# A hybrid SSD / attention / MoE block in fp32: where mean squares are summed, in which order a norm's three small steps run, and how the router's logits are formed

## The chip, the cores and the metric

One NeuronCore of a Trainium2 chip runs the whole program; all arithmetic shown is fp32 unless marked bf16. The metric is the device time of one execution in microseconds. Engines are named as the profile does: PE is TensorE, DVE VectorE, ACT ScalarE, POOL GpSimd, and SP is SyncE, which here only issues DMAs.

## The reference, cut to what matters

Two layers work on 256 latent and 256 context tokens of width 1024. Layer 0 has an SSD (state space) mixer, layer 1 an attention mixer; each is followed by a mixture of experts with 16 experts, a shared expert and a router. Before every mixer and every MoE stands a norm with modulation, so there are four: layer 0 before SSD, layer 0 before MoE, layer 1 before attention (these three on 512 tokens), layer 1 before MoE (256 tokens).

```python
def rmsnorm(x, w):
    y = xf * lax.rsqrt(jnp.mean(xf * xf, axis=-1, keepdims=True) + EPS)
...
m_l = modulate(rmsnorm(h, norm2_w[l]), sh2, sc2)        # x * (1 + scale) + shift
h = h + g2 * grouped_moe(m_l, router_w, ...)
...
scores = jax.nn.sigmoid((t @ router_w).astype(jnp.float32))      # router_w is [1024, 16]
# group and expert choice from scores + bias, top 2 experts of a token
out = swiglu(t, sh_gate, sh_up, sh_down)                          # the shared expert
for e in range(N_EXPERTS):
    out = out + combine[:, e:e + 1] * swiglu(t, w_gate[e], w_up[e], w_down[e])
```

## The kernel before, in words

Activations lie transposed: `hT` (the residual) and `aT` (the normed input) are [128 channels, 8 blocks k, tokens]. Each engine has its own instruction stream, written out by hand, and they meet at semaphores only. Weights stream from HBM through ten slots of 1 MB, issued by SP in a fixed order; SP waits for a slot to be given back before it loads it again.

**A norm.** `norm_modulate` on ACT (L732) squares the eight blocks of `hT` into `aT` as they become ready (L737). `mean_square` on PE (L1052) multiplies each squared block by a 128x128 matrix of 1/1024 and sums the eight in one PSUM bank: eight fp32 matmuls of 128x512 (128x256 in the last norm), each shown as two instructions. `norm` on DVE (L1671) adds EPS out of PSUM (L1673) and takes the reciprocal (L1674); ACT takes the square root (L739); DVE multiplies each block of `hT` by the result (L1677), and ACT applies scale and shift per block (L744, one instruction for each 256 tokens), counted by `s_a`.

**What comes ahead of each norm.** Ahead of norm 1 (layer 0, MoE) PE projects the mixer's output in eight chunks m of 16 matmuls (L1297), and DVE adds each chunk to `hT` (L1878, L1880). Ahead of norm 3 (layer 1, MoE) it is the attention's output projection, L1614 and L2132. Ahead of norm 2 (layer 1, attention) the MoE's result is turned back by PE (L1431) and added to `hT` by DVE block by block (L2067); PE waits for all eight blocks (L1500) before it starts the eight mean-square matmuls in bank 7.

**The front of a MoE** (`moe_pe`, L1304; `moe_act`, L919; `moe_dve`, L2015). For each tile t of 128 tokens PE makes the router logits with eight matmuls: a block of `aT` is stationary (128x128), the router's 16 columns move (L1311). ACT takes the sigmoid (L932, with a table load), and DVE works through some fifty small linked steps, `route`, L1885, up to `s_sel`. Meanwhile PE runs the shared expert's `hidden_chunk(0, 0)` (gate in r = 0, up in r = 1, eight matmuls each, L1333) on weights that arrived long before, turns `aT` for the gathers (L1443), runs `hidden_chunk(0, 1)`, waits for `s_sel`, counts the ranks of the chosen tokens (L1451), and so on through two more chunks, between which DVE works out the order of the experts, a flag (L1972) and the gather indices (L1978 to L1991).

**After the front.** POOL gathers rows of tokens for each of the 16 experts, PE multiplies them in tiles of 32 rows in four column groups (L1379, L1409), and SP streams 6 MB of weights for each expert. In layer 0 SP loads no expert before the flag; in layer 1 one is loaded ahead, and the next when `hidden_chunk(0, 3)` gives the shared expert's slots back. After the last expert PE computes the shared expert's down projection (L1423).

Of the kernel before, what the change touches and what calls it, by code (L numbers as in the profile page):

```python
# [26 lines left out]
P = 128  # L27
# [176 lines left out]
def build(nc, a, out):  # L204
# [24 lines left out]
    with ExitStack() as ctx:  # L229
# [44 lines left out]
        cparts = sb("cparts", [P, 2, T], BF16)  # L274
        small = sb("small", [P, 16])
        ps = ctx.enter_context(nc.psum_tensor("ps", [P, 8, 512], F32))

# [99 lines left out]
        s_op, s_h1 = sem("out_proj"), sem("h_plus_mixer")  # L377
        s_rl, s_rs1 = sem("router_logits"), sem("router_sigmoid")
        s_gu, s_sg, s_hid, s_sd, s_hT, s_yn4, s_yu = (
# [213 lines left out]
        def _(pool):  # L593
            pool.memset(ones[:, :], 1.0).then_inc(s_set, 1)
            pool.memset(mean[:, :], 1.0 / D).then_inc(s_set, 1)
            pool.memset(cs[:, :, :], 0.0).then_inc(s_set, 1)

            pool.wait_ge(s_const, 16 * n_consts)
# [75 lines left out]
            def moe_pool(l):  # L674
# [6 lines left out]
                with pool.If(sparse):  # L681
# [14 lines left out]
                    for s in range(NE):  # L696
# [4 lines left out]
                        if s:  # L701
# [6 lines left out]
                            .then_inc(s_scat[l], 16)  # L708

            moe_pool(0)  # L710
            moe_pool(1)

        @block.scalar
        def _(act):
# [10 lines left out]
            act.wait_ge(s_par, 1)  # L725
            act.wait_ge(s_set, 3)
            act.activation(cs[:, :, 0:2], par[:, 296:312].rearrange("p (c k) -> p k c", c=2), ACT.Silu).then_inc(s_par, 1)
# [3 lines left out]

            def norm_modulate(l, m, n, ready):  # L732

                i = 2 * l + m
                for k in range(KD):
                    ready(k)
                    act.activation(aT[:, k, 0:n], hT[:, k, 0:n], ACT.Square).then_inc(s_sq, 1)  # L737
                act.wait_ge(s_rs, 2 * i + 1)
                act.activation(rstd[:, 0:n], rstd[:, 0:n], ACT.Sqrt).then_inc(s_rs, 1)  # L739
                act.wait_ge(s_mod, AMOD_N[l, m])  # L740
                for k in range(KD):
                    act.wait_ge(s_nx, KD * i + k + 1)
                    for q in range(n // S):
                        ins = act.activation(aT[:, k, q * S:(q + 1) * S], aT[:, k, q * S:(q + 1) * S], ACT.Identity,  # L744
                                             bias=mod[:, l, 24 * m + k, q:q + 1], scale=amod[:, l, m, k, q:q + 1])
                    ins.then_inc(s_a, 1)
# [6 lines left out]

            norm_modulate(0, 0, T, ready0)

# [15 lines left out]
            def conv_in(i):  # L771
                act.wait_ge(s_ip, i + 1)
                if i >= 2:
                    act.wait_ge(s_conv, i - 1)
                else:
                    act.wait_ge(s_set, 9)
                bank = i % 2 if i < AHEAD else 0
                act.copy(pre[i % 2][:, :, PADS:PADS + S], ps[:, bank, :].rearrange("p (s n) -> p s n", s=2)).then_inc(s_pre, 1)
# [140 lines left out]
            def moe_act(l):  # L919
                n = TOK[l]  # L920
                nt = n // P

                def chunk(e, f):
                    q = KF * e + f
                    act.wait_ge(s_gu[l], q + 1)
                    if q >= 2:
                        act.wait_ge(s_hid[l], q - 1)
                    act.activation(sg[f % 2][:, 0:n], ps[:, 2 * (f % 2), 0:n], ACT.Silu).then_inc(s_sg[l], 1)

                act.dma_start(valf[l], a["val"][l]).then_inc(s_val, 16)  # L930
                act.wait_ge(s_rl, l + 1)
                act.activation(rt[0][:, 0:nt * NE], ps[:, 6, 0:nt * NE], ACT.Sigmoid).then_inc(s_rs1, 1)  # L932
                chunk(0, 0)

                for r in range(2 * nt):
                    act.wait_ge(s_mt8, 8 * l + r + 1)
                    act.copy(mtok[:, r // 2, :].rearrange("p (k c q) -> p k c q", k=KD, c=KD)[:, :, 4 * (r % 2):4 * (r % 2) + 4, :],
                             ps[:, (4, 7)[r % 2], :].rearrange("p (c q k) -> p k c q", c=4, k=KD)).then_inc(s_mtv, 1)
                act.wait_ge(s_mtv, 8 * l + 2 * nt)
                act.dma_start(m_rows[0:n, :].rearrange("(t p) n -> p t n", p=P), mtok[:, 0:nt, :]).then_inc(s_mr, 16)  # L940
                for f in range(1, KF):
                    chunk(0, f)
                sparse = choose(act, l)
                with act.If(sparse):
                    rowsT_act(l, 0)
                    for s in range(NE):
                        tiled_act(l, s)
                    act.wait_ge(s_scat[l], 16 * NE)
                    act.wait_ge(s_dn[l], NE)
                    act.wait_ge(s_hT[l], NE)  # L950
                    pairs = y_rows[l].rearrange("(k t p) n -> p t k n", k=2, p=P)
                    for t in range(nt):
                        act.dma_start(ypair[:, t, :, :], pairs[:, t, :, :]).then_inc(s_yp[l][t], 16)
                with act.Else():
# [4 lines left out]
            norm_modulate(0, 1, T, lambda k: act.wait_ge(s_h1, k + 1))  # L959
            moe_act(0)  # L960

            norm_modulate(1, 0, T, lambda k: act.wait_ge(s_h2, k + 1))

# [36 lines left out]
            act.activation(esk, esk, ACT.Exp).then_inc(s_sum, 1)  # L1000
            norm_modulate(1, 1, S, lambda k: act.wait_ge(s_h1, KD + k + 1))
            act.dma_start(fnw, a["final_norm_w"].partition_broadcast(P)).then_inc(s_fw, 16)
# [12 lines left out]
        def _(pe):  # L1015
# [36 lines left out]
            def mean_square(i, n, bank):  # L1052
                for k in range(KD):
                    pe.wait_ge(s_sq, KD * i + k + 1)
                    ins = pe.matmul(ps[:, bank, 0:n], mean[:, :], aT[:, k, 0:n], start=(k == 0), stop=(k == KD - 1))  # L1055
                ins.then_inc(s_ms, 1)

            pe.wait_ge(s_set, 2)
# [159 lines left out]

            pe.wait_ge(s_set, 9)
            pe.wait_ge(s_cT, 3)  # L1220
# [67 lines left out]
            for m in range(KD):  # L1288
# [10 lines left out]
                if m == 0:  # L1299
                    pe.wait_ge(s_ssq, KI)  # L1300
                    pe.wait_ge(s_b3v, len(B3))
                    pe.matmul(ps[:, 3, :], mean[:, :], ssq[:, :], start=True, stop=True).then_inc(s_rsy, 1)

            def moe_pe(l):  # L1304
                n = TOK[l]
                nt = n // P
                for t in range(nt):
                    for k in range(KD):
                        if t == 0:
                            pe.wait_ge(s_a, KD * (2 * l + 1) + k + 1)  # L1310
                        ins = pe.matmul(ps[:, 6, t * NE:(t + 1) * NE], aT[:, k, t * P:(t + 1) * P], rw[:, k, :],  # L1311
                                        start=(k == 0), stop=(k == KD - 1))
                ins.then_inc(s_rl, 1)

# [8 lines left out]
                def hidden_chunk(e, f):  # L1323
# [7 lines left out]
                    for r in range(2):  # L1331
                        for k in range(KD):
                            ins = pe.matmul(ps[:, 2 * (f % 2) + r, 0:n], pair_slot(unit(e, k // 2))[:, k % 2, r, f * P:(f + 1) * P],  # L1333
                                            aT[:, k, 0:n], start=(k == 0), stop=(k == KD - 1))
# [159 lines left out]


            mean_square(1, T, 3)
            moe_pe(0)


            pe.wait_ge(s_h2, KD)  # L1500
            mean_square(2, T, 7)
            pe.wait_ge(s_a, 3 * KD)
# [102 lines left out]
            for m in range(KD):  # L1605
# [10 lines left out]
                ins.then_inc(s_ao, 1)  # L1616
            mean_square(3, S, 0)
            pe.wait_ge(s_h1, 2 * KD)
# [11 lines left out]
        def _(dve):  # L1630
# [48 lines left out]
            norm(0, T, 7)  # L1679
            ada_rows(0)  # L1680
# [190 lines left out]
            for m in range(KD):  # L1871
# [7 lines left out]
                for q in range(2):  # L1879
                    ins = dve.scalar_tensor_tensor(out=hT[:, m, q * S:(q + 1) * S], in0=yb[m % 2][:, q * S:(q + 1) * S],  # L1880
                                                   scalar=mod[:, 0, 16 + m, q:q + 1], in1=hT[:, m, q * S:(q + 1) * S],
                                                   op0=ALU.mult, op1=ALU.add)
                ins.then_inc(s_h1, 1)

            def route(l):  # L1885
# [15 lines left out]

                dve.wait_ge(s_rs1, l + 1)
                link(dve.tensor_tensor(e3(1), e3(0), rb[:, :].unsqueeze(1).to_broadcast([P, nt, NE]), ALU.add))
# [167 lines left out]

            norm(1, T, 3)
            moe_dve(0)

            norm(2, T, 7)

# [57 lines left out]
            norm(3, S, 0)  # L2134
            moe_dve(1)
# [34 lines left out]
```

## Time and profile before

| what | us |
|---|---|
| median of 3 runs | 1641.71 (1639.67 to 1646.81) |
| the profiled execution, own time | 1640.55 |
| its span | 1638.4 |
| PE busy | 1445.5 (88%) |
| DVE busy | 518.5 (32%) |
| ACT busy | 378.3 (23%) |
| POOL busy | 187.7 (11%) |

Shares by engine of the chain that ended last: PE 72%, SP's queue 9%, DMA 7%, DVE 5%, ACT 5%. The page also gives the clock that PE was granted in each fortieth of the span (a 9 is full speed or nearly; a 5 is half):

```profile
PEclk9599989999989999979999999997999899999987
```

The chain is followed back from the last instruction, at each step to what released it. So an engine that is busy but not in the chain costs nothing there, and the busy share says nothing about a single stage. The chain and the instructions in time are the views to read for a change that touches short stretches only.

### The profile page before, as it was taken

What the parts mean: (1) busy time and instruction counts of PE and PEld (TensorE: products, weight loads), DVE (VectorE), ACT (ScalarE), POOL (GpSimd) and SP (SyncE); (2) the same over time, 40 slices, a digit from 0 to 9 for tenths busy, and PEclk for the clock granted to TensorE, in tenths of its full rate; (3) what the DMA queues carried; (4) which work ended last, traced back from release to release, by engine and by line L of the source; (5) the groups of instructions that cost most, each with busy time, mean ns of one, the idle gap of its engine ahead of it and who ended that gap; (6) DMA issues with size and microseconds to landing.
All of it is one profiled execution on the core that took longest, in us unless ns stands there. A gap on an engine that the chain in (4) does not pass through costs nothing.

```text
span 1638.4 us, 28948 instructions
## 1 busy us (share of the span) xinstructions
PE 1445.5 (88%) x12440; PEld 832.2 (51%) x12440; DVE 518.5 (32%) x918; ACT 378.3 (23%) x900; POOL 187.7 (11%) x207
## 2 busy tenths in 40 slices
PE   4799989899988999899999998996988999988766
PEld 2433445454544444365555555552845775554424
DVE  3255555544443221224121121132244331211103
ACT  2211334333424210130121121113053212211111
POOL 0000033223242200000011111000000000111100
PEclk9599989999989999979999999997999899999987
DMA  7355314344340442003999999990400349999992
GB/s 280 126 183 202 128 65 149 125 139 141 120 138 26 110 122 77 26 25 129 389 370 373 384 392 381 378 323 2 142 26 4 116 139 352 393 397 399 403 392 100
DMA packets 128132, 334.46 MB, mean 204 GB/s; under 512 B 13123, under 2 KB 60923, under 8 KB 121851
## 3 DMA queue, kind: packets, MB, share of 16 engines
q1 hardware_dynamic: 116027, 308.76, 51.8%
q0 software_dynamic: 6144, 12.60, 2.3%
q10 hardware_dynamic: 5824, 11.16, 1.9%
q8 instruction: 101, 1.65, 0.4%
q14 instruction: 36, 0.29, 0.1%
HBM read 325.65 MB, written 14.68 MB: 208 GB/s over the span
## 4 chain that ended last, share of the span: by engine, by line
PE 72%; SPq 9%; DMA 7%; DVE 5%; ACT 5%; issue 2%; DVEq 0%; ACTq 0%; POOLq 0%
PE ps L1379 12%; PE ps L1085 10%; PE ps L1102 7%; PE ps L1297 7%; SPq L517 6%; PE ps L1409 5%; PE ps L1333 4%; PE ps L1036 3%; PE ps L1423 3%; SPq L519 2%; PE ps L1190 2%; DMA ssb<-in_moe_w_up 2%; PE ps L1614 2%; PE ps L1526 2%; PE ps L1055 2%
## 5 line engine op out<-in xcount | busy, mean ns | idle before, releaser
L1379 PE MATMUL ps<-ring,ssb 128*32 128x256 f32 x2960 | 174.3, 383 | 14.4 <-DMA ring<-in_moe_w_up 12.0
L1085 PE MATMUL ps<-aT,ring 128*128 128x512 f32 x384 | 175.1, 605 | 0.0
L1379 PEld LDWEIGHTS ps<-ring,ssb 128*32 128x32 f32 x2960 | 106.0, 110 | 77.8 <-DMA ring<-in_moe_w_up 15.8
L2012 DVE COPY big<-ps 32x256 f32<-32x256 f32 x160 | 67.7, 423 | 180.8 <-PE ps L1409 179.1
L1085 PEld LDWEIGHTS ps<-aT,ring 128*128 128x128 f32 x384 | 71.6, 193 | 84.1 <-issue 84.0
L1102 PE MATMUL ps<-aT,ring 128*128 128x512 f32 x256 | 114.2, 595 | 0.0
L1297 PE MATMUL ps<-big,ring 128*128 128x512 f32 x256 | 110.2, 592 | 0.0
L2005 DVE TENSOR_TENSOR ssb<-ssb,ps 128x256 f32<-128x256 f32 (+3 forms) x32 | 15.6, 488 | 270.8 <-ACT ssb L907 270.8
L1409 PE MATMUL ps<-ring,ssb 128*32 128x256 f32 x1472 | 87.1, 389 | 13.6 <-ACT ssb L911 9.7
L816 ACT ACTIVATE ssb<-ps,ncum 128x128 f32<-128x128 f32 x256 | 73.3, 371 | 98.7 <-PE ps L1165 97.9
L916 ACT COPY big<-ps 32x256 f32<-32x256 f32 x160 | 58.0, 362 | 160.3 <-PE ps L1409 158.8
L1333 PE MATMUL ps<-aT,ring 128*128 128x512 f32 (+1 forms) x256 | 89.3, 509 | 0.0
L1297 PEld LDWEIGHTS ps<-big,ring 128*128 128x128 f32 x256 | 48.6, 190 | 61.2 <-issue 61.0
L907 ACT ACTIVATE ssb<-ps 128x256 f32<-128x256 f32 (+3 forms) x32 | 14.0, 438 | 265.5 <-PE ps L1379 265.5
L1102 PEld LDWEIGHTS ps<-aT,ring 128*128 128x128 f32 x256 | 47.2, 190 | 52.6 <-issue 52.6
L1744 DVE SCALAR_TENSOR_TENSOR ring<-ring,par 128x512 f32<-128x512 f32 x96 | 72.8, 759 | 3.4
L1379 PE MATMUL ps<-ssb 128*32 128x256 f32 x1104 | 66.6, 387 | 7.1 <-DMA ssb<-in_moe_w_up 6.3
L1409 PEld LDWEIGHTS ps<-ring,ssb 128*32 128x32 f32 x1472 | 46.2, 111 | 48.7 <-ACT ssb L911 14.4
L1379 PE MATMUL ps<-tmp,ssb 128*32 128x256 f32 x1056 | 62.7, 380 | 6.7 <-DMA tmp<-in_moe_w_up 6.1
L706 POOL DMA_INDIRECT y_rows<-big,sidx x32 | 30.1, 939 | 335.7 <-DVE big L2012 305.8
L1333 PEld LDWEIGHTS ps<-aT,ring 128*128 128x128 f32 x256 | 50.5, 200 | 34.3 <-issue 30.8
L1036 PE MATMUL ps<-ring,cs 128*32 128x512 f32 x384 | 55.3, 657 | 5.7 <-DMA ring<-in_ada_w 5.7
(288 smaller groups left out, 1854.0 us busy)
## 6 DMA issues: line engine op xcount, KB each, us to landing
ring<-in_ada_w SPq DMA_DIRECT2D x48, 1024.0 KB
ring<-in_moe_w_gate SPq DMA_DIRECT2D x75, 512.0 KB
ring<-in_moe_w_up SPq DMA_DIRECT2D x75, 512.0 KB
ring<-in_moe_w_down SPq DMA_DIRECT2D x37, 1024.0 KB
ring<-in_ssd_in_w SPq DMA_DIRECT2D x20, 1024.0 KB
tmp<-in_moe_w_down SPq DMA_DIRECT2D x14, 1024.0 KB
ssb<-in_moe_w_gate SPq DMA_DIRECT2D x27, 512.0 KB
ssb<-in_moe_w_up SPq DMA_DIRECT2D x27, 512.0 KB
```

The source lines that it names most:

```text
L517: sp_.dma_start(pair_slot(u)[:, :, r, :], src).then_inc(s_w[u.slot], 16)
L816: ins = act.activation(E[:, h, :], ps[:, 5, j * P:(j + 1) * P], ACT.Exp, bias=ncum[:, t, col:col + 1])
L916: ins = act.copy(Y[s % 2][32 * g:32 * g + 32, 256 * c:256 * c + 256], tiled_y[32 * c:32 * c + 32, g, :])
L1036: ins = pe.matmul(ps[32 * j:32 * j + 32, 2, :], cs[:, k, :], ring[:, u.slot, 512 * j:512 * j + 512], start=(k == 0), stop=(k == KD - 1))
L1085: ins = pe.matmul(ps[:, bank, :], slot(u)[:, k, (i % 2) * P:(i % 2 + 1) * P], aT[:, k, :], start=(k == 0), stop=(k == KD - 1))
L1102: ins = pe.matmul(ps[:, z_bank(i), :], slot(u)[:, k, (i % 2) * P:(i % 2 + 1) * P], aT[:, k, :], start=(k == 0), stop=(k == KD - 1))
L1297: ins = pe.matmul(ps[:, 4 + m % 4, :], w[:, k, :], xT[:, k, :], start=(k == 0), stop=(k == KI - 1))
L1333: ins = pe.matmul(ps[:, 2 * (f % 2) + r, 0:n], pair_slot(unit(e, k // 2))[:, k % 2, r, f * P:(f + 1) * P], aT[:, k, 0:n], start=(k == 0), ...
L1379: ins = pe.matmul(tiled_gu[32 * c:32 * c + 32, g, :].rearrange("p (r n) -> p r n", r=2), XgT[l][:, k * C + 32 * g:k * C + 32 * g + 32], pa ...
L1409: ins = pe.matmul(tiled_y[32 * c:32 * c + 32, g, :], hiddenT[l][:, g, 32 * k:32 * k + 32], slot(u, 2)[:, k % 2, c * UC:(c + 1) * UC], star ...
L1744: ins = dve.scalar_tensor_tensor(out=o, in0=pre[i % 2][:, :, tap:tap + S], scalar=par[:, tap * NCONV + ch:tap * NCONV + ch + 1], in1=o, op ...
L2012: ins = dve.tensor_copy(Y[s % 2][32 * g:32 * g + 32, 256 * c:256 * c + 256], tiled_y[32 * c:32 * c + 32, g, :])
```

## The change

Four edits.

1. In every norm, EPS is no longer added by DVE: ACT takes the square root straight out of PSUM with EPS as its bias, then DVE takes the reciprocal.
2. In norms 1 and 3, DVE adds the squared blocks 0 to 6 into `ssq` as they appear, between its additions to `hT`; PE multiplies that sum and block 7 only: two matmuls in place of eight.
3. In norm 2, PE waits for each squared block and no longer for all of `hT`, and uses bank 0.
4. The router: weights padded to 32 columns (`rw32`, built by POOL over `dt`'s memory during the output projection) are stationary, and `aT` moves, block k going to column group k % 4, so that four partial sums stand in 32 partitions each. ACT copies them to SBUF; four small matmuls (two in layer 1) against `four`, the sum of four slices of the identity, add and turn them to tokens by experts. PE does r = 0 of `hidden_chunk(0, 0)` first, waiting for each modulated block; the partial logits come ahead of r = 1, their sums after its k = 1 (layer 0) or k = 3 (layer 1).

```diff
+        rw32 = dt[:, :, :].rearrange("p t n -> p (t n)").rearrange("p (k e) -> p k e", k=KD)
+        four = ncum[:, 0, 0:NE]
...
+            pool.memset(small[:, 15:16], EPS).then_inc(s_set, 1)
...
+            pool.wait_ge(s_h1, 1)
+            pool.memset(rw32[:, :, :], 0.0).then_inc(s_rw, 1)
+            pool.wait_ge(s_rw, 1)
+            pool.tensor_copy(rw32[:, :, 0:NE], rw[:, :, :]).then_inc(s_rw, 1)
+            pool.tensor_tensor(four, ident[:, 0:NE], ident[:, 32:32 + NE], ALU.add).then_inc(s_rw, 1)
+            for c in range(2, 4):
+                pool.wait_ge(s_rw, c + 1)
+                pool.tensor_tensor(four, four, ident[:, 32 * c:32 * c + NE], ALU.add).then_inc(s_rw, 1)
...
-                act.wait_ge(s_rs, 2 * i + 1)
-                act.activation(rstd[:, 0:n], rstd[:, 0:n], ACT.Sqrt).then_inc(s_rs, 1)
+                act.wait_ge(s_ms, i + 1)
+                act.activation(rstd[:, 0:n], ps[:, bank, 0:n], ACT.Sqrt, bias=small[:, 15:16]).then_inc(s_rs, 1)
...
-                act.wait_ge(s_rl, l + 1)
-                act.activation(rt[0][:, 0:nt * NE], ps[:, 6, 0:nt * NE], ACT.Sigmoid).then_inc(s_rs1, 1)
+                act.wait_ge(s_rl, 2 * l + 1)
+                act.copy(ssq[:, 0:n], ps[:, 6, 0:n]).then_inc(s_rs1, 1)
+                act.wait_ge(s_rl, 2 * l + 2)
+                act.activation(rt[0][:, 0:nt * NE], ps[:, 5, 0:nt * NE], ACT.Sigmoid).then_inc(s_rs1, 1)
...
+            def mean_square_of_sum(i, n, bank, summed):
+                pe.wait_ge(s_ssq, summed)
+                pe.matmul(ps[:, bank, 0:n], mean[:, :], ssq[:, 0:n], start=True, stop=False)
+                pe.wait_ge(s_sq, KD * (i + 1))
+                pe.matmul(ps[:, bank, 0:n], mean[:, :], aT[:, KD - 1, 0:n], start=False, stop=True).then_inc(s_ms, 1)
...
-                for t in range(nt):
+                def logit_parts():
+
                     for k in range(KD):
-                        if t == 0:
-                            pe.wait_ge(s_a, KD * (2 * l + 1) + k + 1)
-                        ins = pe.matmul(ps[:, 6, t * NE:(t + 1) * NE], aT[:, k, t * P:(t + 1) * P], rw[:, k, :],
-                                        start=(k == 0), stop=(k == KD - 1))
-                ins.then_inc(s_rl, 1)
+                        c = k % 4
+                        ins = pe.matmul(ps[32 * c:32 * c + 32, 6, 0:n], rw32[:, k, :], aT[:, k, 0:n], start=(k < 4), stop=(k >= 4))
+                    ins.then_inc(s_rl, 1)
+
+                def logit_sums():
+
+                    pe.wait_ge(s_rs1, 2 * l + 1)
+                    for t in range(nt):
+                        ins = pe.matmul(ps[:, 5, t * NE:(t + 1) * NE], ssq[:, t * P:(t + 1) * P], four, start=True, stop=True)
+                    ins.then_inc(s_rl, 1)
...
                         for k in range(KD):
+                            if q == 0 and r == 0:
+                                pe.wait_ge(s_a, KD * (2 * l + 1) + k + 1)
+                            if q == 0 and r == 1 and k in (0, 2 * l + 2):
+                                (logit_sums if k else logit_parts)()
...
-            mean_square(1, T, 3)
+            mean_square_of_sum(1, T, 3, KI + 1)
             moe_pe(0)
...
+            mean_square(2, T, 0)
             pe.wait_ge(s_h2, KD)
-            mean_square(2, T, 7)
...
-            mean_square(3, S, 0)
+            mean_square_of_sum(3, S, 0, KI + 2)
...
-            def norm(i, n, bank):
-                dve.wait_ge(s_ms, i + 1)
-                link(dve.tensor_scalar(rstd[:, 0:n], ps[:, bank, 0:n], EPS, None, ALU.add))
+            def add_squares(i, k, n):
+                dve.wait_ge(s_sq, KD * i + k + 1)
+                if k == 1:
+                    link(dve.tensor_tensor(ssq[:, 0:n], aT[:, 0, 0:n], aT[:, 1, 0:n], ALU.add))
+                elif k < KD - 2:
+                    link(dve.tensor_tensor(ssq[:, 0:n], ssq[:, 0:n], aT[:, k, 0:n], ALU.add))
+                else:
+                    dve.tensor_tensor(ssq[:, 0:n], ssq[:, 0:n], aT[:, k, 0:n], ALU.add).then_inc(s_ssq, 1)
+
+            def norm(i, n):
+                dve.wait_ge(s_rs, 2 * i + 1)
                 dve.reciprocal(rstd[:, 0:n], rstd[:, 0:n]).then_inc(s_rs, 1)
...
                 ins.then_inc(s_h1, 1)
+                if 1 <= m < KD - 1:
+                    add_squares(1, m, T)
```

## Rows read from the trace of the kernel before

**Rows 1.** The page, 40 slices of 41 us: busy tenths of the 16 DMA engines.
```profile
DMA  7355314344340442003999999990400349999992
```

**Rows 2.** Chain that ended last, layer 0's MoE front: start us, us, what.
```profile
681.85 6.88 PE ps L1055 x16
688.75 0.70 DVE rstd L1673
689.48 3.36 DVE rstd L1674
692.86 0.64 ACT rstd L739
...
694.31 7.98 ACT aT L744 x16
702.34 10.85 PE ps L1311 x50
713.19 15.43 PE ps L1333 x32
...
747.32 2.14 PE ps L1451 x20
...
771.56 10.46 DMA ssb<-m_rows,gidx
```

**Rows 3.** VectorE's instructions in time: start us, us, engine line op, [idle before].
```profile
681.88 0.69 DVE L1878 TENSOR_TENSOR tmp<-ps,rstd 128x512 f32<-128x512 f32 x1 [12.12 <-PE ps L1297]
...
720.71 0.23 DVE L1935 TENSOR_TENSOR tmp<-tmp 128x64 f32<-128x64 f32 x1
```

**Rows 4.** ScalarE's instructions in time, the last square of layer 0's second norm.
```profile
683.53 0.63 ACT L737 ACTIVATE aT<-hT 128x512 f32<-128x512 f32 x1 [13.11 <-DVE hT L1880]
```

**Rows 5.** One line: op xcount, ns min/median/max, first and last start, forms.
```profile
L739 ACT ACTIVATE rstd<-rstd x4: 416/629/630, 34.7 to 1294.5; 128x512 f32<-128x512 f32 x3, 128x256 f32<-128x256 f32 x1
L739 ACT ACT_TABLE_LOAD  x3: 1283/1283/1283, 27.0 to 1289.8; - x3
...
L744 ACT ACTIVATE aT<-aT,mod,amod x56: 583/587/602, 49.6 to 1299.0; 128x256 f32<-128x256 f32 x56
```

**Rows 6.** TensorE's instructions in time, four column groups of 32, 512 columns moving.
```profile
30.52 3.64 PE L1036 MATMUL ps<-ring,cs 128*32 128x512 f32 x32
```

**Rows 7.** Windows of 1 us: PE busy (instructions), granted clock, DMA share, GB/s.
```profile
692.00:693.00 1.00, 0.00 (x0) 0.68 0.00 0
716.00:717.00 1.00, 1.00 (x3) 0.87 0.00 0
1105.00:1106.00 1.00, 0.00 (x0) 0.69 0.70 223
1112.00:1113.00 1.00, 1.00 (x3) 0.90 0.00 0
```

**Rows 8.** Chain, layer 1's first norm.
```profile
1102.23 6.37 DVE hT L2067 x16
1108.64 8.90 PE ps L1055 x16
```

**Rows 9.** Chain, layer 1's second norm and MoE front.
```profile
1288.81 3.47 PE ps L1055 x16
1292.30 0.43 DVE rstd L1673
1292.76 1.76 DVE rstd L1674
...
1296.65 6.97 PE ps L1311 x30
1303.62 8.61 PE ps L1333 x32
```

**Rows 10.** SyncE's DMA issues in time, the first that follow each router.
```profile
765.25 0.36 SPq L517 DMA_DIRECT2D ring<-in_moe_w_gate  x1
...
1337.42 0.36 SPq L517 DMA_DIRECT2D ring<-in_moe_w_gate  x1
```

More of the change, by code:

```diff
@@ L377, in build @@
         s_op, s_h1 = sem("out_proj"), sem("h_plus_mixer")
-        s_rl, s_rs1 = sem("router_logits"), sem("router_sigmoid")
+        s_rl, s_rs1, s_rw = sem("router_logits"), sem("router_sigmoid"), sem("router_weights")
         s_gu, s_sg, s_hid, s_sd, s_hT, s_yn4, s_yu = (
@@ L725, in _ @@
             act.wait_ge(s_par, 1)
-            act.wait_ge(s_set, 3)
+            act.wait_ge(s_set, 4)
             act.activation(cs[:, :, 0:2], par[:, 296:312].rearrange("p (c k) -> p k c", c=2), ACT.Silu).then_inc(s_par, 1)
@@ L730, in _, with norm_modulate @@
                 act.copy(hT[:, k, :], ps[:, (k + 1) % 8, :]).then_inc(s_ha, 1)
-            def norm_modulate(l, m, n, ready):
+            def norm_modulate(l, m, n, bank, ready):
                 i = 2 * l + m
@@ L752, in ready0 @@
                     act.wait_ge(s_hd, k // 2 + 1)
-            norm_modulate(0, 0, T, ready0)
+            norm_modulate(0, 0, T, 7, ready0)
             act.wait_ge(s_sp, 3)
@@ L775, in conv_in @@
                 else:
-                    act.wait_ge(s_set, 9)
+                    act.wait_ge(s_set, 10)
                 bank = i % 2 if i < AHEAD else 0
@@ L957, in moe_act @@
                             chunk(e, f)
-            norm_modulate(0, 1, T, lambda k: act.wait_ge(s_h1, k + 1))
+            norm_modulate(0, 1, T, 3, lambda k: act.wait_ge(s_h1, k + 1))
             moe_act(0)
-            norm_modulate(1, 0, T, lambda k: act.wait_ge(s_h2, k + 1))
+            norm_modulate(1, 0, T, 0, lambda k: act.wait_ge(s_h2, k + 1))
             act.wait_ge(s_kv, 1)
@@ L1000, in _ @@
             act.activation(esk, esk, ACT.Exp).then_inc(s_sum, 1)
-            norm_modulate(1, 1, S, lambda k: act.wait_ge(s_h1, KD + k + 1))
+            norm_modulate(1, 1, S, 0, lambda k: act.wait_ge(s_h1, KD + k + 1))
             act.dma_start(fnw, a["final_norm_w"].partition_broadcast(P)).then_inc(s_fw, 16)
@@ L1217, in _ @@
                     turn_x(i - 2)
-            pe.wait_ge(s_set, 9)
+            pe.wait_ge(s_set, 10)
             pe.wait_ge(s_cT, 3)
@@ L1302, in _ @@
                     pe.matmul(ps[:, 3, :], mean[:, :], ssq[:, :], start=True, stop=True).then_inc(s_rsy, 1)
+            pe.wait_ge(s_rw, 5)
             def moe_pe(l):
@@ L1677, in norm @@
                     dve.tensor_tensor(aT[:, k, 0:n], hT[:, k, 0:n], rstd[:, 0:n], ALU.mult).then_inc(s_nx, 1)
-            norm(0, T, 7)
+            norm(0, T)
             ada_rows(0)
@@ L1900, in tg @@
                     return rt[i][:, 0:4 * nt].rearrange("p (t g) -> p t g", g=4)
-                dve.wait_ge(s_rs1, l + 1)
+                dve.wait_ge(s_rs1, 2 * l + 2)
                 link(dve.tensor_tensor(e3(1), e3(0), rb[:, :].unsqueeze(1).to_broadcast([P, nt, NE]), ALU.add))
@@ L2070, in moe_dve @@
                     ins.then_inc(s_h2, 1)
-            norm(1, T, 3)
+            norm(1, T)
             moe_dve(0)
-            norm(2, T, 7)
+            norm(2, T)
             tabs = [v.unsqueeze(1).to_broadcast([P, 2, S]) for v in (cosT, sinT)]
@@ L2133, in _ @@
                                          in1=hT[:, m, 0:S], op0=ALU.mult, op1=ALU.add).then_inc(s_h1, 1)
-            norm(3, S, 0)
+                if 1 <= m < KD - 1:
+                    add_squares(3, m, S)
+            norm(3, S)
             moe_dve(1)
```

## The prediction

> **What bounds the kernel now.** I read the page first, for the stages. The DMA engines are full in two stretches, the experts of layer 0 (slices 18 to 26) and of layer 1 (slices 33 to 39), and nearly idle ahead of each [rows 1]. So each MoE consists of a front, in which no expert weights stream, and a body bound by the weights of its 16 experts. The reader is to see the low digits ahead of each run of nines. A change ahead of a body can't shorten it, but can start it earlier. Which of the two happens is told by SP's issues in time: the first load of layer 0's experts goes out at 765.25, right behind the router's flag, and in layer 1 the stream goes on at 1337.42, when the shared expert's fourth chunk is over [rows 10]. Both hang on the front. So time saved in a front should be saved at the end, and I worked out the fronts from the chain of waits, then from the instructions in time, the source lines, and windows of 1 us for the clock.
>
> The four norms: that of layer 0's mixer isn't on the path, since ACT's modulation waits for the ada weights (its first instruction starts at 49.6, while the square root starts at 34.7) [rows 5]: I count 0 there, for every edit. The other three are on it.
>
> **Prices.** An fp32 matmul of 512 columns takes 6.88 / 8 = 0.86 us at 2.4 GHz, one of 256 columns 3.47 / 8 = 0.43 [rows 2, 9]. At 1.2 GHz I take double; chunk(0, 0) of layer 0 bears it out: it starts at 713.19, the clock rises at 716.1, and 1.7 matmuls at 1.72 and 14.3 at 0.86 give 15.2 against 15.43 measured [rows 2, 7].
>
> **Layer 0's MoE front.** (a) Mean square. The output projection ends at 681.85, and then eight matmuls run although only the last block is late: DVE starts on it at 681.88, and its square ends at 684.16 [rows 2 to 4]. After the change PE does the matmul of the sum by 682.7, waits for that square, and needs 0.86 and some 0.25 to wake and drain (estimate): 685.3 in place of 688.73. (b) EPS. The DVE addition goes, 0.70 and a handover of 0.03 [rows 2]. The root gets a bias operand. No row has a root with one; a 128x256 instruction with two such operands takes 587 ns, one with none 416 [rows 5], so one costs between 0 and 0.17; I take 0.09, since two are the 0.17. Root 685.3 to 686.0, reciprocal 3.36, first multiplication at 689.5 in place of 693.52: **4.0 saved**. The table load of the root does not come into it in this norm: there are three for four roots, and none lies between the square and the root here [rows 5].
>
> (c) The order of PE's work. Before: eight modulated blocks (694.31 to 702.3), then 10.85 of router, nearly all of it 1.2 GHz, then 15.43 of chunk(0, 0): it ends at 728.6 [rows 2]. After: the first modulated block is there at 690.3 + 1.0 + 0.15 = 691.4, the last at 698.3. PE has been idle since 685.3, and after the idle time from 688.75 the clock fell at 692.3, 3.6 us later [rows 2, 7]; so I count r = 0 from its start at 1.2 GHz. At 1.72 each it is slower than ACT at 1.0 a block, so it is busy without a gap and should get its clock back as in the rows: 2.9 us after 713.19, and 3.5 us after 1108.64 [rows 2, 7, 8]. With 3.6: 2.1 matmuls, then 5.9 at 0.86, r = 0 ends at 700.1. Bounds: at full clock throughout it is bound by ACT and ends at 699.3; at half throughout, 705.2. Partial logits: the ada matmuls, 128x32 stationary and 512 moving in four column groups, are 16 in 3.64 us [rows 6], so eight take 1.8; bounds 1.8 and, side by side not at all, 6.9. Then k = 0 and 1 of r = 1 (1.7) to 703.6; ACT's copy of the partial logits, about 0.6 like its other 512 columns [rows 4], and a table load of 1.28 if one follows it [rows 5], end by 703.9, and the sigmoid needs them only at 704.5. The four sums move 16 columns; 25 such matmuls took 10.85 at half clock [rows 2], so 0.22 each at full, 0.9 together. The last six matmuls, 5.2, and the drain: 709.8. **18.8 saved**, the 4.0 within.
>
> What is late next? The new waits are of the sums for ACT's copy (behind them the rest of r = 1; the copy is done 0.9 earlier), and of the sum's matmul for DVE's sixth addition. Those additions, 0.69 each, lie in DVE's idle time of 12.1 us per chunk [rows 3], behind a square of 0.63; the next `hT` addition stands behind them and isn't due for 10 us. Without that cover they would cost 6 x 0.7 = 4.2. Routing now starts at about 704.8 and needs 7.4 to `s_sel` (713.4 to 720.9) [rows 2, 3]: 712.2, while PE asks for it behind chunk(0, 1), before at 747.32, now at 728.5. So routing had 26 us to spare and keeps 16. All behind goes on as before: rank, flag, indices, the gather of 10.46 [rows 2]. POOL's five steps (memset, copy, three additions) start 90 us ahead; at 5 us together by any row they are hidden. SP's queue isn't passed by anything and none of its waits moves, other than by what it waits for.
>
> The Trainium skill would make one step dearer ("TensorE: Matmul & The Clock Gate", Measured speedup vs the span model): four tiles side by side are measured there at 3.07 times one, not four. By it the eight would take 2.2 and the sum here and in layer 1 would be 0.6 worse. The ada row is of this very form and shows the full factor of four, so the sum goes by it.
>
> **Layer 1's first norm.** Before, PE starts when all of `hT` is there, 1108.64, and needs 8.90, partly at half clock: it had fallen at 1105.4 and came back at 1112.1 [rows 7, 8]. After, the first `hT` block is done at 1103.0, its square at 1103.8, the first matmul starts at 1103.9; blocks come every 0.80 [rows 8], PE at 0.86 is the slower: done at 1111.0 in place of 1117.54, 6.6 less. The EPS step gives 0.7 less the 0.1 of the bias: **7.2 saved**. It is idle for only 1.5 us, so I count full clock; if it falls all the same at 1105.4 and for 3.5 us, that costs 1.7, and half clock for all eight 6.9. Attention's own start waits for all modulated blocks in both kernels, and shifts along.
>
> **Layer 1's second norm and front.** PE's eight matmuls end at 1292.28 [rows 9]. The last square, started with 0.42 right before the third table load (its start is the 1289.8), and the matmul would be done at 1290.5; but that table load of 1.28 ends at 1291.1, and here it is the later [rows 5]. Root, reciprocal 1.76, first multiplication at 1293.4 in place of 1295.0: **1.6 saved**. PE starts r = 0 at 1294.6 in place of its router at about 1296.3. At half clock for 3.6 us (4.2 matmuls at 0.86), then 3.8 at 0.43: 1299.8. Partial logits 0.9, four matmuls of r = 1 1.7, two sums 0.4, four more 1.7, drain 0.1: 1304.7. Before, the router ended at 1303.6 and chunk(0, 0) at 1312.23 [rows 9]: **7.5 saved**, the 1.6 within. Routing itself starts only a little earlier, at 1303.1 and not 1303.9, and is at most 7.4 long, so done by 1310.5; PE comes for it no sooner than 6.9 (chunk(0, 1)) behind 1304.7 and the turns of `aT` between them, at 1311.6 or later: at least 1 us to spare.
>
> The skill has a rule against this edit ("ScalarE: Activation LUTs", What ACT_TABLE_LOAD costs): a switch of tables costs a drain besides the load, 2.66 us. By that the root of this norm would start at 1292.5 and the saving shrink by 1.4. The trace disagrees: the load starts in the 20 ns behind the square, and is 1283 ns.
>
> **Sum.** 18.8 + 7.2 + 7.5 = 33.5. The profiled execution took 1640.55 (span 1638.4), so 1607.0. The median is 1641.71, 0.07% above, within which the runs differ anyway (0.4%). I forecast **1607**.
>
> **Rivals.** First, *the streams do not follow.* If a body's end were fixed by something that does not hang on its front, only the 7.2 of attention's norm would be left: 1633.3. For it: the bodies are at full DMA rate [rows 1]. Against: their first issues [rows 10].
>
> Second, *the clock stays down through chunk(0, 0).* If r = 0, which starts cold and then alternates with other forms, does not get the clock back before the chunk is over: layer 0 16 x 1.72 + 3.6 + 1.8 from 691.4 ends at 724.4, 14.6 later than forecast; layer 1 16 x 0.86 + 2.7 from 1294.6, 1311.1, 6.4 later: 1628. For it: small router matmuls kept it at half for 14 us while PE was busy [rows 2, 7]. Against: shared-expert matmuls bring it back within 3 us.
>
> Third, *column groups one after the other:* 6.9 in place of 1.8, and 3.4 in place of 0.9: 1614.6. Against it [rows 6]; for it only that in the new form every block has its own moving data read by one quarter of the array, which is so in the ada form as well.
>
> Fourth, *slower:* the clock stays at 1.2 GHz through all four shared chunks of both fronts. To the 21.0 above come 48 x 0.86 = 41 and 48 x 0.43 = 21: 1690. It decides against the change from about 39 matmuls of 512 columns at half clock beyond those counted. Only a clock that no longer answers to dense matmuls would do that, and no row shows it.
>
> **How the numbers follow.** Forecast, with its bounds, 0.75; clock down in the chunk 0.09; column groups in series 0.07; streams do not follow 0.06; slower 0.03. The range runs from 1600 (r = 0 bound by ACT in both layers, 1.3 less, the waking and draining estimates gone, run to run differences) to 1620, which takes in the serial groups and the cold starts that cost up to 5.1 + 1.5 + 1.7. About 0.5% (8.2 us) is what a measurement here can tell from no change. The rival of the streams lies right at that bound, and half of it counts as the same: faster 0.94, same 0.03, slower 0.03.
>
> **What would show it.** Per step: mean square of norm 1 ends 3.4 after the output projection, first multiplication at 7.7 after it; no L1673; chunk(0, 0) of layer 0 over 28.0 after the output projection's end (46.8 before); eight partial logits in 1.8; first expert load of layer 0 at about 746.5; the attention norm's eight matmuls 8.8 from the first `hT` block to their end; chunk(0, 0) of layer 1 over 15.9 after the attention's output (23.4 before); the bodies unchanged in length. Wrong it would be if a body grew by what its front lost, if PE waited for `s_sel` or in the sums, or if windows at r = 0 and r = 1 showed 1.2 GHz beyond 4 us.

## The result, and the profile after

1614.78 us median of 4 runs (1613.29 to 1618.33) against 1643.61 of the kernel before beside them (1639.67 to 1646.81): ratio 0.9823, 95% interval 0.9803 to 0.9842, so 28.8 us or 1.8% faster. The forecast was 1607 with a range of 1600 to 1620. The profiled execution took 1616.23 (span 1614.1), 24.3 less than the one of before, which at 1640.55 was 3.1 below its median; a difference between single profiles carries run to run differences of some us.

The table cuts both profiled executions at the same events (end of the last matmul of a group, start of the next); "forecast" is before less what the prediction takes off in that stage.

| stage, us | before | forecast | after |
|---|---|---|---|
| start to the end of layer 0's output projection | 681.8 | 681.8 | 683.2 |
| to the turns of `aT` (chunk(0, 0) is over) | 46.6 | 27.8 | 28.6 |
| to the first routed matmul of layer 0 | 55.5 | 55.5 | 53.6 |
| body of layer 0, to the first addition to `hT` | 318.2 | 318.2 | 318.8 |
| norm 2, to the first matmul of the keys | 28.9 | 21.7 | 26.7 |
| keys | 16.4 | 16.4 | 17.0 |
| attention, to its output projection | 113.3 | 113.3 | 114.5 |
| its output projection | 27.9 | 27.9 | 30.0 |
| norm 3 and chunk(0, 0) of layer 1, to its turns | 23.3 | 15.8 | 17.4 |
| to the first routed matmul of layer 1 | 28.6 | 28.6 | 28.7 |
| body of layer 1 | 281.1 | 281.1 | 280.6 |
| the end | 16.6 | 16.6 | 14.9 |

**Layer 0's front.** The chain that ended last, after, over the stretch of [rows 2] (start us, us, what). The reader is to see that L1673's addition is gone, that two matmuls stand where eight did, that r = 0 (L1364 x16) starts right behind the first modulated block, and that the router is down to 1.85 (partial logits, L1332) and 0.80 (sums, L1339) inside the chunk:

```profile
685.58 1.14 PE ps L1075 x2
...
686.75 0.70 ACT rstd L750
...
687.47 3.36 DVE rstd L1713
...
690.85 0.70 DVE aT L1716
...
691.64 1.10 ACT aT L755 x2
...
692.88 9.28 PE ps L1364 x16
702.16 1.85 PE ps L1332 x16
704.02 1.91 PE ps L1364 x4
705.93 0.80 PE ps L1339 x8
706.73 5.26 PE ps L1364 x12
...
730.69 2.14 PE ps L1482 x20
```

ScalarE's instructions in time there: the copy of the partial logits, the sigmoid's table load behind it, and the sigmoid 0.8 us after that, so the load is hidden by 0.8:

```profile
704.08 0.58 ACT L943 COPY ssq<-ps 128x512 f32<-128x512 f32 x1 [4.47 <-PE ps L1332]
704.69 1.28 ACT L945 ACT_TABLE_LOAD   x1
706.77 0.22 ACT L945 ACTIVATE tmp<-ps 128x64 f32<-128x64 f32 x1 [0.80 <-PE ps L1339]
```

Windows of 1 us after (PE busy, granted clock, DMA share, GB/s), beside [rows 7]: the clock fell at 687.0 and rose at 697.3, 4.4 us after r = 0 had begun.

```profile
687.00:688.00 1.00, 0.00 (x0) 0.52 0.00 0
697.00:698.00 1.00, 1.00 (x3) 0.86 0.30 100
```

**Norm 2.** TensorE's instructions in time after. In brackets is the idle time before. The eight matmuls, which should have followed the squares, start 4.62 us after the last turning matmul, though the first square was ready at 1085.8; the chain names the fifth square only because it is the last that had come by then:

```profile
1077.18 7.31 PE L1462 MATMUL ps<-c,big 128*128 128x128 f32 x64
1089.12 8.83 PE L1068 MATMUL ps<-aT,mean 128*128 128x512 f32 x16 [4.62 <-ACT aT L748]
```

```profile
1089.00:1090.00 1.00, 0.88 (x2) 0.90 0.11 28
1090.00:1091.00 1.00, 1.00 (x2) 0.50 0.00 0
1093.00:1094.00 1.00, 1.00 (x4) 0.89 0.00 0
```

The clock falls at 1089.8, just behind that idle time, and comes back at 1093.2. Before, the same eight started at 1108.64 and took 8.90 [rows 8]; after, 8.83.

**Layer 1's front.** The chain after, beside [rows 9]. The root waits for its table load, as forecast; r = 0 takes 6.66, of which 6.0 at half clock.

```profile
1273.49 1.28 ACT L750
1274.79 0.48 ACT rstd L750
...
1278.35 6.66 PE ps L1364 x16
1285.01 1.00 PE ps L1332 x16
1286.01 1.93 PE ps L1364 x8
1287.93 0.35 PE ps L1339 x4
1288.28 1.82 PE ps L1364 x8
```

**The end of attention.** Windows of 2 us after: TensorE is busy with small matmuls (32 rows) and loses its clock ahead of the output projection; the row of the chain is that projection's, 29.96 for the 128 that took 27.82 before.

```profile
1238.49:1240.49 2.00, 2.00 (x38) 0.88 0.04 8
1240.49:1242.49 2.00, 2.00 (x21) 0.50 0.00 0
```

```profile
1242.56 29.96 PE ps L1645 x128
```

### The profile page after: what moved, and what is told of

It reads as the page before. It is cut to its first block, busy times and chain, and to the rows that moved or that the text cites. A ratio compares the mean times of both kernels' runs of the same rounds, so it can differ in the third digit from the quotient of the medians.

```text
span 1614.1 us, 28822 instructions
## 1 busy us (share of the span) xinstructions
PE 1419.9 (88%) x12364; PEld 799.9 (50%) x12364; DVE 523.3 (32%) x926; ACT 378.8 (23%) x902; POOL 188.7 (12%) x213
## 4 chain that ended last, share of the span: by engine, by line
PE 70%; SPq 10%; DMA 8%; DVE 5%; ACT 4%; issue 3%; DVEq 0%; ACTq 0%; POOLq 0%
PE ps L1104 11%; PE ps L1410 10%; PE ps L1121 7%; PE ps L1316 7%; SPq L519 7%; PE ps L1440 5%; PE ps L1364 5%; DMA ring<-in_moe_w_up 4%; SPq L521 3%; PE ps L1049 3%; PE ps L1454 3%; PE ps L1209 2%; PE ps L1645 2%; PE ps L1557 2%; PE ps L1157 2%
## 5 line engine op out<-in xcount | busy, mean ns | idle before, releaser
L1410 PE MATMUL ps<-ring,ssb 128*32 128x256 f32 x2960 | 168.8, 381 | 21.7 <-DMA ring<-in_moe_w_up 20.1
L1410 PEld LDWEIGHTS ps<-ring,ssb 128*32 128x32 f32 x2960 | 97.7, 110 | 88.6 <-DMA ring<-in_moe_w_up 23.7
L1440 PE MATMUL ps<-ring,ssb 128*32 128x256 f32 x1472 | 89.0, 394 | 13.8 <-ACT ssb L922 9.9
L1364 PE MATMUL ps<-aT,ring 128*128 128x512 f32 (+1 forms) x256 | 90.5, 512 | 10.3 <-ACT aT L755 10.3
L1364 PEld LDWEIGHTS ps<-aT,ring 128*128 128x128 f32 x256 | 50.7, 202 | 45.6 <-issue 41.0
L1440 PEld LDWEIGHTS ps<-ring,ssb 128*32 128x32 f32 x1472 | 46.5, 113 | 50.4 <-ACT ssb L922 14.5
```

What stands on the lines that cost most here:

```text
L1410: ins = pe.matmul(tiled_gu[32 * c:32 * c + 32, g, :].rearrange("p (r n) -> p r n", r=2), XgT[l][:, k * C + 32 * g:k * C + 32 * g + 32], pa ...
L1440: ins = pe.matmul(tiled_y[32 * c:32 * c + 32, g, :], hiddenT[l][:, g, 32 * k:32 * k + 32], slot(u, 2)[:, k % 2, c * UC:(c + 1) * UC], star ...
```

## The experiments

All times are medians. Each group ran on one chip beside the kernel before: the first four with it at 1643.19, the next four at 1645.88, the last two at 1643.68.

| run | us | ratio to before, 95% |
|---|---|---|
| after_again | 1615.73 | 0.9829, 0.9810 to 0.9847 |
| ms2_in_branch | 1607.53 | 0.9782, 0.9759 to 0.9805 |
| ms2_after_all | 1617.68 | 0.9838, 0.9819 to 0.9857 |
| router_as_before | 1636.42 | 0.9951, 0.9933 to 0.9969 |
| idle_matmul | 1614.98 | one run |
| keep_busy | 1601.93 | 0.9735, 0.9716 to 0.9754 |
| eight_mean_squares | 1616.47 | 0.9831, 0.9810 to 0.9852 |
| one_column_group | 1623.80 | one run |
| short_else | 1607.47 | 0.9783, 0.9758 to 0.9808 |
| no_branch | 1606.15 | 0.9774, 0.9752 to 0.9796 |

**after_again**, the changed kernel unaltered.

> The changed kernel once more, as the yardstick of this group. Both theories: 1613 to 1618 us, about 0.982 of the kernel before. It also shows what stays the same from run to run: if the 4.6 us in which TensorE stands still between the last turning matmul of layer 0's MoE and its first mean-square matmul (with a squared block ready 3.3 us earlier) is there again, it is no accident of one run; the clock's low stretches of 3 to 6 us may lie elsewhere.

The gap is there again: its mean-square matmuls begin 4.4 us after the last turning matmul, and take 9.41.

```profile
1079.93 5.26 PE ps L1462 x47
...
1085.99 2.45 DVE hT L2108 x6
...
1089.58 9.41 PE ps L1068 x16
```

**ms2_in_branch.** The edit, in both arms of the branch:

```diff
                     turn_sum(lambda t: pe.wait_ge(s_acc[l], 2 * t + 2))
+                    if l == 0:
+                        mean_square(2, T, 0)
...
-            mean_square(2, T, 0)
             pe.wait_ge(s_h2, KD)
```

> The changed kernel, but the eight mean-square matmuls of layer 1's first norm are issued at the end of either arm of the branch (routed and dense path), not behind it. Theory A: TensorE came late because its instructions behind the branch, past the whole dense arm, had to be fetched after the jump while the DMA queues were full of weights; then the first of these matmuls starts 0.2 us behind the first square, the eight end 9 us after the first addition to hT started (13.7 in the changed kernel), and the time falls by 4 to 6 us against the changed kernel. Theory B (the wait itself, or PSUM bank 0 held by something else, holds TensorE up): nothing changes, within 1 us, and the gap of 4.6 stays.

TensorE's instructions in time:

```profile
1076.32 7.31 PE L1462 MATMUL ps<-c,big 128*128 128x128 f32 x64
1084.95 7.13 PE L1068 MATMUL ps<-aT,mean 128*128 128x512 f32 x16 [1.32 <-ACT aT L748]
```

The first one follows the first square, and the eight take 7.13 at full clock: they end 8.7 after the first addition to `hT` (8.8 was forecast, 13.7 was measured in the changed kernel). Theory A holds, B falls. The gain of 8.2 is more than the 4 to 6 expected. In the profiles of this run and of after_again the stages from norm 2 on account for as much: start 1.9, matmuls 2.3, keys 0.7, and 3.3 in attention, where this run doesn't lose the clock. (The two profiles are 11.6 apart; the rest lies in the stretch ahead of layer 0's front, in the bodies and, 0.4, in layer 1's front, which the edit doesn't touch.)

**ms2_after_all**, the third edit undone (and ACT reads bank 7 again):

```diff
-            mean_square(2, T, 0)
             pe.wait_ge(s_h2, KD)
+            mean_square(2, T, 7)
```

> The changed kernel with its third edit undone: in layer 1's first norm TensorE waits for all of hT again and uses bank 7. Theory A (the gap is paid either way): the matmuls start 6.4 us after the first addition to hT and end about 15.3 after it, against 13.7: 1 to 2 us slower than the changed kernel. As first forecast, with the edit worth its full 6.6, it would be 6.6 slower.

1617.68, 2.0 more than after_again, with overlapping intervals; the profile has the matmuls start 6.4 after the first addition and take 9.41. So the edit as it stood was worth 2 to 3 in the norm by the profiles, not 6.6, and the medians can't tell it from nothing:

```profile
1087.86 6.37 DVE hT L2108 x16
...
1094.28 9.41 PE ps L1068 x16
```

**router_as_before**, the fourth edit undone (lines L1307 to L1313 and L932 of the kernel before put back, no waits in r = 0).

> The changed kernel with its fourth edit undone: router weights moving, 32 (16 in layer 1) small matmuls ahead of chunk(0, 0). By the prediction's terms the router's part is 18.8 - 4.0 = 14.8 us in layer 0 and 7.5 - 1.6 = 5.9 in layer 1, so this would be 20.7 slower than the changed kernel; by the trace after, 14.0 + 4.2 and some clock, so 18 to 20 slower. If instead the norm edits carry most of the gain (rival), it is within 8 of the changed kernel.

20.7 slower than after_again, the number that the prediction's terms give. That it fits to the tenth is luck: by stages it is 14.4 in layer 0's front and 5.4 in layer 1's, 19.8 together against 20.7 forecast, and 1.7 in a chunk further on (below). The rival falls: the router's order carries about three quarters of the gain.

**idle_matmul**, a probe behind the branch:

```diff
+            pe.wait_ge(s_h2, 1)
+            pe.matmul(ps[:, 0, :], mean[:, :], ssq[:, :], start=True, stop=True)
             mean_square(2, T, 0)
```

> The changed kernel with one more matmul, whose result nobody uses, directly behind layer 0's branch: it waits only for the first block of hT, not for a square, and goes into bank 0. Theory A (instructions behind the jump arrive late): it starts together with the first mean-square matmul, 4.4 to 4.9 us behind the last turning matmul, and not when the first block of hT is done (0.9 us after the turning ends). Theory B (the wait for the squares holds TensorE up): it starts about 1.0 us behind the last turning matmul, and the mean-square matmuls still at 4.4 to 4.9. Time within 1 us of the changed kernel.

```profile
1077.78 4.96 PE L1462 MATMUL ps<-c,big 128*128 128x128 f32 x43
1087.46 2.08 PE L1532 MATMUL ps<-ssq,mean 128*128 128x512 f32 x2 [4.72 <-DVE hT L2110]
1089.33 8.44 PE L1068 MATMUL ps<-aT,mean 128*128 128x512 f32 x16
```

The probe needs only the first block of `hT`, there at 1084.5, and starts at 1087.46, 4.7 behind the last turning matmul. So it isn't the squares that TensorE waits for. It did not start together with the real ones, as the expectation had it: at half clock it took the 1.9 us between.

**short_else** and **no_branch** tell what behind a branch costs this.

```diff
                 with pe.Else():
-                    for e in range(1, NE + 1):
...
-                    turn_sum(lambda t: None)
+                    shared_down(lambda: None)
```

> The changed kernel, but TensorE's dense arm is cut to its last part, the shared down projection (128 matmuls in layer 0 in place of some 2500 more), so that the jump past it is short; the other engines keep theirs. The arm is not taken with these inputs; its computation would be incomplete if it were. Theory A1 (what is late is the fetch of instructions far behind the jump): the gap between the last turning matmul and the first mean-square matmul shrinks from 4.4 to 4.9 to the 1.7 that the first square needs, or at least to under 3, and the norm ends 4 to 5 us sooner: 1609 to 1612. Theory A2 (any end of a branch costs this): the gap stays at 4.4 or more, 1615.

> The changed kernel with no branch on TensorE at all: it reads no flag and has the routed path only; the other engines keep both. The dense path is left out for TensorE. A1 and A2 both: the gap is 1.7 us (the first square), as in ms2_in_branch, and the time 1608 to 1611. If the gap stays, neither the jump nor the branch is its cause and the wait for the square or the PSUM bank is left.

```profile
1077.98 7.31 PE L1462 MATMUL ps<-c,big 128*128 128x128 f32 x64
1086.80 7.13 PE L1068 MATMUL ps<-aT,mean 128*128 128x512 f32 x16 [1.51 <-ACT aT L748]
```

```profile
1075.66 7.31 PE L1462 MATMUL ps<-c,big 128*128 128x128 f32 x64
1084.70 7.13 PE L1068 MATMUL ps<-aT,mean 128*128 128x512 f32 x16 [1.74 <-ACT aT L748]
```

The counts in the expectation were off: the full arm holds 1600 fp32 matmuls in layer 0, the cut one 32. With the short arm to jump over, TensorE waits for the first square only, 1.5 us idle, as it does without any branch (1.7); and the run is 8.3 us below after_again, 7.6 by the ratios, since the groups differ. In short_else the weights' queue is as full at that moment (window 1086 to 1087: share 1.11; changed kernel 1.13). A1 holds, A2 falls: what counts is how far the jump goes, and not that there is a branch. The Trainium skill says so ("Runtime: NRT & Kernel Launch", Instruction fetch mechanics): an engine's instructions are fetched ahead in sequence, and a taken branch beyond what is held stalls until they have come. It gives no length; here the first matmul comes 4.4 to 4.8 us after the last one ahead of the jump.

The DMA view of the traces shows the transfer too. In all six profiles in which TensorE came late, a transfer of 16 KB on q8, a queue of instructions, begins 1.8 to 2.1 us after the last turning matmul (at 1086.5 in the profile after), and the first matmul behind the jump follows 2.6 us after that beginning, every time. In ms2_in_branch and no_branch no such transfer lies there; in short_else one begins at 2.0, but the first matmul has started by then.

The distance alone does not make the 4.4 to 4.8, though. Layer 1's MoE ends in a branch of the same build, with 1328 matmuls in the arm that is jumped, and there nothing is late. TensorE's instructions in time, the turning matmuls and the last transposes (L1657), and windows around the two jumps (PE busy, granted clock, DMA share, GB/s):

```profile
1597.02 3.73 PE L1462 MATMUL ps<-c,big 128*128 128x128 f32 x32
1602.52 1.97 PE L1657 MATMUL ps<-c,hT 128*128 128x128 f32 x16 [1.76 <-DVE hT L2108]
```

```profile
1086.00:1087.00 1.00, 0.00 (x0) 1.00 1.13 354
1601.00:1602.00 1.00, 0.00 (x0) 1.00 0.00 0
```

The transposes start 1.76 us after the last turning matmul, as soon as `hT` is ready, and so (1.75 to 1.80) in every profile, the kernel before's too. Here the q8 transfer begins at 1599.6, 1.2 ahead of the last turning matmul's end and not 2.0 behind it. What differs between the two places is that the DMA engines carry weights at the first and nothing at the second. That the full queues delay the fetch fits this; no run empties them at the first jump, so it is not shown.

**eight_mean_squares**, the second edit undone (`mean_square(1, T, 3)` and `mean_square(3, S, 0)` again, no `add_squares`).

> The changed kernel with its second edit undone: in the norms ahead of both MoEs TensorE multiplies all eight squared blocks again, and VectorE adds none. By the prediction's terms the sums are worth 3.4 us in layer 0 and, because of the table load, 1.2 in layer 1 (mean square ends at 3.5 in place of 2.3 us after the projection), 4.6 together: 1619 to 1621. Rival (a longer unbroken run of TensorE's keeps its clock a little longer and gives some back): 2 to 3 slower only.

1616.47 in another group than after_again, ratio 0.9831 against 0.9829: no difference that the runs can tell, so the expectation of 4.6 is not borne out. The profile shows both halves. In layer 0 the projection's end to the turns takes 31.8 against 28.6, which is 3.2 of the 3.4. In layer 1 it takes 17.4 against 17.4:

```profile
1273.76 3.62 PE L1068 MATMUL ps<-aT,mean 128*128 128x256 f32 x16
1280.97 5.46 PE L1364 MATMUL ps<-aT,ring 128*128 128x256 f32 x16 [3.59 <-ACT aT L755]
```

The longer mean square costs 1.2, but TensorE has then been idle for 3.59 only and r = 0 takes 5.46 and not 6.66: the clock, low for 3.4 us of r = 0 and not for 6.0, gives back the 1.2. That the 3.2 of layer 0 don't show in the medians stays open; the intervals, 0.2% or 3 us each way, would hide them.

**one_column_group:** `ps[0:32, 6, 0:n]` for all eight k, and the sums with 32 rows.

> The changed kernel with the partial logits of all eight blocks in one column group of 32 instead of four, summed in PSUM. If column groups work side by side, the eight matmuls take 6.9 us in layer 0 and 3.4 in layer 1 in place of 1.85 and 1.00, and the end of chunk(0, 0) moves by 5.0 and 2.4: some 7.5 us slower, 1623. If the array works on one group's matmul at a time and the gain had another source, they take the same as in the changed kernel.

TensorE in time, layer 0 and layer 1, beside 1.85 and 1.00 in four groups:

```profile
703.48 7.05 PE L1331 MATMUL ps<-aT,dt 128*32 128x512 f32 x16
```

```profile
1289.67 3.64 PE L1331 MATMUL ps<-aT,dt 128*32 128x256 f32 x16
```

7.05 and 3.64: four groups at once are 3.8 and 3.6 times one. The turns come 5.3 and 2.8 later, 8.1 us together; the third rival's mechanism, produced on purpose, costs about what was priced (7.6).

**keep_busy.** ms2_in_branch with unused matmuls in three gaps:

```diff
+            def keep_busy(count, n, bank):
+                for _ in range(count):
+                    pe.matmul(ps[:, bank, 0:n], mean[:, :], ssq[:, 0:n], start=True, stop=True)
...
             mean_square_of_sum(1, T, 3, KI + 1)
+            keep_busy(6, T, 0)
...
                         mean_square(2, T, 0)
+                        keep_busy(13, T, 1)
...
             mean_square_of_sum(3, S, 0, KI + 2)
+            keep_busy(8, S, 1)
```

> ms2_in_branch with matmuls whose results nobody uses put into three gaps of TensorE, to keep its clock: 6 of 512 columns behind the mean square of layer 0's second norm (5.2 of the 6.2 us gap), 13 behind that of layer 1's first norm (11.2 of 13.0), 8 of 256 columns behind that of layer 1's second (3.5 of 4.1). If the half clock at the start of the next stage comes from these gaps, the windows there show 1.0 throughout: r = 0 of layer 0 takes 7.9 instead of 9.3 us (then ScalarE's pace of 1.0 a block binds), the first keys' matmuls 13.8 instead of 16.3, r = 0 of layer 1 4.8 instead of 6.7: together 5.8, so 1600 to 1603 us against 1607.5 for ms2_in_branch. Rival: the added matmuls delay the real ones or the clock falls all the same: no gain, or 1 to 3 us slower.

```profile
686.79 5.31 PE L1073 MATMUL ps<-ssq,mean 128*128 128x512 f32 x12
693.12 7.92 PE L1368 MATMUL ps<-aT,ring 128*128 128x512 f32 x16 [1.02 <-ACT aT L755]
```

```profile
1105.11 13.97 PE L1548 MATMUL ps<-aT,ring 128*128 128x512 f32 x32 [1.85 <-issue]
```

```profile
1266.14 4.05 PE L1368 MATMUL ps<-aT,ring 128*128 128x256 f32 x16 [0.67 <-ACT aT L755]
```

r = 0 takes 7.92 (9.28 in the changed kernel), the keys 13.97 (16.30 in ms2_in_branch), r = 0 of layer 1 4.05 (6.66). None was held up: each starts behind an idle time of 0.67 to 1.85. One thing went the other way: norm 2's own mean square took 8.79 for the 7.13 of ms2_in_branch. In this run the first addition to `hT` started 1.0 us after the last turning matmul and not 0.3 ahead of its end, TensorE was idle for 2.6 us, and the clock fell at 1083.3, just as the matmuls began:

```profile
1083.00:1084.00 1.00, 0.69 (x1) 0.63 0.98 308
```

So the gaps that were filled no longer cost clock, and one that was not filled did. The time, 1601.93, is in the range expected; this is the fastest kernel here, 2.65% below the kernel before, against the changed one's 1.77% below.

## Why the prediction was right, and where it was not

**The streams follow their fronts.** Right: the bodies took 318.8 and 280.6 against 318.2 and 281.1, and in all ten experiments 317.2 to 320.2 and 280.2 to 282.9, wherever they began. The first rival is out, and with it the reading that a stage at full DMA rate can't be gained on.

**Layer 0's mean square and EPS.** 4.0 forecast; the first multiplication comes 7.6 us after the projection's end in place of 11.7: 4.1. The root with a bias took 0.70 against 0.64, so the bias cost 0.06 where 0.09 was put.

**Layer 0's order.** 18.8 forecast, 18.0 measured. Partial logits 1.85 (1.8), sums 0.80 (0.9), r = 0 9.28 (8.7), because the clock stayed low for 4.4 us and not 3.6. All new waits were hidden as forecast. 1.9 more came where nothing was forecast: chunk(0, 2) took 13.83 and not 15.53. It is no sure gain of the change: short_else, idle_matmul and eight_mean_squares, which hold the same change there, took 15.53. But the other six experiments with the new router order took 13.83, and both profiles with the old order (before, router_as_before) 15.53; whether the change makes the shorter time more frequent is not shown.

**Norm 2: the step that failed.** "its square at 1103.8, the first matmul starts at 1103.9". 7.2 were forecast; 2.2 were saved up to the keys, and 1.6 are left of them behind the keys, which took 0.6 longer. The prediction took the wait that had been removed for the only thing that held TensorE. Behind it stood the jump over the dense arm, 4.4 to 4.8 us, which the old wait of 6.2 had covered. And since TensorE then stood still, the clock fell after all, which the text had priced (1.7) and thought unlikely. ms2_in_branch, short_else and no_branch each bring the forecast 8.8 back.

**Layer 1's front.** 7.5 forecast, 5.9 measured. The 1.6 of the norm was 1.6 (root at 1274.79, 2.3 behind the projection, held by the table load). The term mis-sized is r = 0: 6.66 against 5.2, with a low clock of 6.0 us from its first matmul against 3.6. keep_busy, with r = 0 at full clock in 4.05, shows that the clock is the whole of it.

**Attention** took 3.3 more in the profile after, not in the prediction at all: clock lost at its end. It came in all runs in which the mean square of norm 2 was late, in router_as_before only in part (1.7), but not in the kernel before, where it was late too. What triggers it was not isolated, so of the 8.2 that ms2_in_branch gains, these 3.3 go with the gap but are not shown to come from it.

**The sum.** 33.5 forecast, 24.3 in the profiles, 28.8 between the medians. From 33.5: norm 2 and the keys 5.6 less, attention 3.3, layer 1's front 1.6, layer 0's 0.8, the stretch ahead of it 1.4 and the bodies 0.1 (not forecast, run to run): 12.8 less. 1.9 (the chunk) and 1.7 (the end, where TensorE before stood 1.3 us in the middle of its last transposes without a wait) came on top. That stop, too, comes with a q8 transfer: it begins at 1625.3, and the transposes go on at 1627.7. The range held because its upper end had been set for cold clocks and serial groups, not for this cause. That much is luck, and so are the 3.6 that nobody had forecast.

**The rivals.** Column groups in series: no, 1.85. The 3.07 that the prediction quotes is the Trainium skill's figure for four row tiles, and these are column tiles; one_column_group measures 3.8 for them. Clock down through the chunk: no, it rose within r = 0. Slower: no.

**Readings of the rows that were a little off.** Counted from 0, the slices with full DMA engines are 19 to 26 and 33 to 38, not 18 to 26 and 33 to 39. The windows' means put the clock's return at 716.3 and 1112.2, not 716.1 and 1112.1. Neither changes the sum.

## What to carry to other kernels

Before a wait is counted as removed, ask what else had to happen in its shade: here the fetch of instructions behind a long jump. Work that has to start promptly goes inside the arm of a branch, not behind it, unless it has to wait longer than the fetch anyway. And a forecast for TensorE after an idle stretch needs the granted clock of that stretch: 4 to 6 us of half clock were paid at three places, and matmuls that nobody needs, put into a gap that they do not overrun, took them away there.

## What had not been expected of the hardware

- Behind a jump over 1600 matmuls TensorE started 4.4 to 4.8 us after its last matmul, 2.6 after the beginning of an instruction transfer, in six profiles (after, after_again, idle_matmul, router_as_before, eight_mean_squares, one_column_group); behind one over 32 (short_else) after the 1.5 that the data took. Behind a jump over 1328 with idle DMA queues it started after the 1.8 that the data took, in all ten profiles that have this jump.
- Two edits that each shorten TensorE's path do not add up through the clock: in layer 1's norm 1.2 us of mean square saved were paid back by 1.2 of slower r = 0.
- Four column groups of 32 with four different moving operands ran at 3.8 times one group's rate at 512 columns, 3.6 at 256.
